# Seven block products for eight in the first output projection of a two-layer trunk kernel

## The reference

```python
# layer 0: y is the Fourier-mixed half of the input projection, z the other half
y = jnp.fft.fft2(ug, axes=(1, 3), norm='ortho').real.reshape(b, l, D_BRANCH)
o = (y * jax.nn.silu(z)) @ w_out            # (768 tokens x 2048) @ (2048 x 1024)
x = x + gt_l * o                            # ctx the same, with gt_c
# layer 1
h = rmsnorm(x, norm_g) * (1.0 + sc) + sh    # needs the sum over all 1024 features of x
q, k, v, z = split(h @ w_in)                # four heads; q and z of the latent tokens only
```

## Time and profile before

| | us |
|---|---|
| median of the runs | 947.4 |
| lowest of the runs | 945.88 |
| the profiled execution | 944.97 |
| its span, first to last instruction | 943.2 |
| PE busy in the span | 924.1 |
| granted PE clock, mean | 0.997 |

### The profile page before, as it was taken

One profiled execution on the slowest core, in us unless ns is written; L12 is line 12 of the kernel. 1 busy time (PEld: TensorE's weight loads), 2 busy tenths in 40 slices (PEclk: granted clock), 3 DMA queues, 4 the chain that ended last, 5 costly groups with the idle time before them and its releaser, 6 DMA issues.

```text
span 943.2 us, 13109 instructions
## 1 busy us (share of the span) xinstructions
PE 924.1 (98%) x4835; PEld 801.5 (85%) x4835; DVE 546.9 (58%) x813; ACT 351.0 (37%) x598; POOL 240.2 (25%) x243
## 2 busy tenths in 40 slices
PE   6999999999999999999999999999999999999996
PEld 6999998888888888888888888888888888888886
DVE  6897869999974422367444444435435445468333
ACT  8353343242232322354323334424323333354223
POOL 5259941746563000014100220012100221011001
PEclk9999999999999999999999999999999999999998
DMA  9762324555545212212211122202121121102222
GB/s 365 287 223 90 113 93 153 191 189 179 195 162 223 65 48 67 90 45 90 86 52 42 44 90 67 68 1 89 67 67 44 44 70 63 58 9 90 90 90 89
DMA packets 28747, 98.78 MB, mean 105 GB/s; under 512 B 3688, under 2 KB 5896, under 8 KB 28448
## 3 DMA queue, kind: packets, MB, share of 16 engines
q1 hardware_dynamic: 26688, 91.10, 28.2%
q0 software_dynamic: 1744, 6.84, 1.9%
q10 hardware_dynamic: 272, 0.26, 0.1%
HBM read 96.07 MB, written 2.10 MB: 104 GB/s over the span
## 4 chain that ended last, share of the span: by engine, by line
PE 89%; DVE 3%; DMA 2%; issue 2%; ACT 2%; POOL 1%; SPq 1%; POOLq 0%; DVEq 0%
PE banks L1725 29%; PE banks L1726 29%; PE banks L1727 29%; DMA raw<-stream 1%; DMA gate<-x_rows 1%; DVE hreg L1246 1%; ACT hreg L919 0%; POOL gate L661 0%; DVE wreg L1200 0%; DVE dist L1210 0%; PE banks L1852 0%; POOL gate L701 0%; DVE ring L1128 0%; PE banks L1870 0%; SPq L440 0%
## 5 line engine op out<-in xcount | busy, mean ns | idle before, releaser
L1725 PE MATMUL banks<-hreg,ring 128*128 128x512 f32 (+2 forms) x940 | 332.2, 353 | 1.9 <-DVE ring L1128 0.9
L1726 PE MATMUL banks<-hreg,ring 128*128 128x512 f32 (+2 forms) x940 | 331.3, 352 | 0.0
L1727 PE MATMUL banks<-hreg,ring 128*128 128x512 f32 (+2 forms) x940 | 329.5, 351 | 0.0
L1110 DVE TENSOR_TENSOR ring<-raw,ring 128x512 fp32r<-128x512 f32 x192 | 141.6, 751 | 244.3 <-ACT ring L713 243.0
L713 ACT ACTIVATE ring<-raw 128x512 fp32r<-128x512 f32 x192 | 118.7, 629 | 362.9 <-PE banks L1727 277.9
L1725 PEld LDWEIGHTS banks<-hreg,ring 128*128 128x128 f32 x940 | 177.3, 189 | 27.0 <-issue 3.6
L1727 PEld LDWEIGHTS banks<-hreg,ring 128*128 128x128 f32 x940 | 176.8, 188 | 22.4
L1726 PEld LDWEIGHTS banks<-hreg,ring 128*128 128x128 f32 x940 | 177.4, 189 | 21.1 <-issue 0.2
L628 POOL TENSOR_TENSOR gate<-xreg,gate 128x257 f32<-128x257 f32 (+1 forms) x64 | 69.2, 1111 | 78.4 <-ACT gate L862 62.2
L1142 DVE CUSTOM_DVE_ANT_0 dist<-raw,gate 128x1024 bf16<-128x1024 f32 x64 | 83.7, 1308 | 3.8
L661 POOL TENSOR_TENSOR gate<-gate 128x512 f32<-128x512 f32 x12 | 17.2, 1430 | 250.7 <-ACT gate L943 249.9
(11 more groups left out here) (230 smaller groups left out, 1095.0 us busy)
## 6 DMA issues: line engine op xcount, KB each, us to landing
raw<-stream SPq DMA_DIRECT2D x148, 512.0 KB, 3.3
gate<-stream SPq DMA_DIRECT2D x10, 512.0 KB, 11.2
gate<-x_rows SPq DMA_DIRECT2D x6, 512.0 KB, 6.8
gate<-x_lat POOLq DMA_DIRECT2D x1, 2048.0 KB, 8.8
xreg<-x_lat POOLq DMA_DIRECT2D x1, 2048.0 KB, 10.7
out<-xreg SPq DMA_DIRECT2D x3, 384.0 KB, 2.6
xreg<-stream SPq DMA_DIRECT2D x2, 512.0 KB, 11.1
gate<-cond_in SPq DMA_DIRECT2D x2, 512.0 KB, 10.8
```

Source lines behind the costliest of these rows:

```text
L1110: dve.tensor_tensor(ring[:, n % 2, 1, c], raw[:, buf, c], f32(ring[:, n % 2, 0, c]), ALU.subtract).then_inc(split_done, 1)
L1725: pe.matmul(out, left[0], right[0], start=start, stop=False)
L1726: pe.matmul(out, left[0], right[1], start=False, stop=False)
L1727: return pe.matmul(out, left[1], right[0], start=False, stop=stop)
```

## The change

Out0 becomes the seven products of Strassen's scheme. The weights are cut in 2 x 2 blocks by the parity of the output tile `m` and of the input tile `kk`. The gated values are cut by the parity of `kk` and by the halves of the 768 columns (384 each, so that the second half has 128 latent columns and all 256 of the context). A product q is the sum or difference of one or two weight blocks (first part of a row in `PRODUCTS`) times the sum or difference of one or two blocks of gated values (`RIGHT`; products 0 and 1 take a block as it is), and its result is added to or taken from one or two blocks of x (second part of the row). Each product has four output tile pairs i, so there are 28 units of one slot each. A unit is 8 `mm3` of 384 columns.

Three things feed a unit:

- **Weights.** Products 2 and 3 have one weight block. For 0, 1, 5 and 6 SP loads the first block and POOL issues a transfer that adds the second to it in the same buffer (`add_weights`). For product 4 the two blocks are loaded into two buffers and POOL subtracts the second from the first in two halves (`subtract_weights`). Then ACT and DVE split as before (`mix_hi`, `mix_lo`).
- **Gated values.** POOL makes 40 sums of 384 columns (`sum_right`) through two small buffers, ACT and DVE split each (`right_hi`, `right_lo`), at the units that `UNIT_STEPS` names: two at an odd one and three at an even one, from unit 3 to unit 18.
- **Results.** DVE adds each unit's result to x in two or more pieces (`evict`), two units later from unit 8 on.

The silu of the last two groups goes to a buffer of its own and group 7 is gated by DVE (`gate_last`). The context columns of x are complete before the latent ones, so their norm runs beside units 26 and 27, and head 0's context keys get two slots (`kc`) and matmuls of their own ahead of the head. Slots 4 and 5 of head 0 then have latent columns only.

```diff
+PRODUCTS = (
+    (((1, 0), (1, 1)), ((1, 0, 1), (1, 1, -1))),
+    (((0, 0), (0, 1)), ((0, 0, -1), (0, 1, 1))),
+    (((0, 0),), ((0, 1, 1), (1, 1, -1))),
+    (((1, 1),), ((0, 0, -1), (1, 0, 1))),
+    (((0, 0), (1, 1)), ((0, 0, 1), (1, 1, -1))),
+    (((0, 0), (1, 0)), ((1, 1, 1),)),
+    (((0, 1), (1, 1)), ((0, 0, 1),)),
+)
...
+RIGHT = {2: ((0, 1), (1, 1), ALU.subtract), 3: ((1, 0), (0, 0), ALU.subtract),
+         4: ((0, 0), (1, 1), ALU.add), 5: ((0, 0), (0, 1), ALU.add), 6: ((1, 0), (1, 1), ALU.add)}
+HOMES = (0, 1, 2, 3, 0, 2, 1)
+STEPS = [(q, i) for q in (2, 3, 4, 6, 5) for i in range(PAIRS)]
+UNIT_STEPS = [[] for _ in range(UNITS)]
+for _n in range(len(STEPS)):
+    UNIT_STEPS[3 + 2 * (_n // 5) + (_n % 5) // 2 - (_n % 5 == 4)].append(_n)
...
+FIRST_ORDER = [(i, k) for part in (range(6), range(6, PAIRS)) for i in range(4) for k in part]
+MIX_BANKS = (6, 7, 0, 1, 2, 3, 4, 5)
+EVICT_AT = {5: (0, 1), 6: (2, 3, 4), 7: (5,), **{_u: (_u - 2,) for _u in range(8, UNITS)}}
...
+            for n, (u, second) in enumerate(RAW_USES):
+                buf, _ = MIX_FIRST[u, second]
+                if n < RAW_BUFS:
+                    sp.wait_ge(split_done, 2 * (SLOT_OUT0 - RAW_BUFS + n) + 2 + SPLIT0)
+                else:
+                    v, was_second = RAW_USES[n - RAW_BUFS]
+                    if was_second:
+                        sp.wait_ge(mix_sum, 2 * (v - 4 * DIFFERENCE) + 2)
+                    else:
+                        sp.wait_ge(split_done, 2 * (SLOT_OUT0 + v) + 2 + SPLIT0)
...
+            def add_weights(u):
+                if u < UNITS and two_slots(u) and u // 4 != DIFFERENCE:
+                    buf, landed = MIX_FIRST[u, 0]
+                    pool.wait_ge(s_raw[buf], landed)
+                    pool.dma_start(raw[:, buf, :], mix_in[MIX_SLOTS.index((u, 1))],
+                                   accum_op=ALU.add).then_inc(s_added[buf], 16)
+            def subtract_weights(u):
+                if u // 4 == DIFFERENCE:
+                    (a, a_landed), (b, b_landed) = MIX_FIRST[u, 0], MIX_FIRST[u, 1]
+                    pool.wait_ge(s_raw[a], a_landed)
+                    pool.wait_ge(s_raw[b], b_landed)
+                    for c in (slice(0, SLOT // 2), slice(SLOT // 2, SLOT)):
+                        pool.tensor_tensor(raw[:, a, c], raw[:, a, c], raw[:, b, c],
+                                           ALU.subtract).then_inc(mix_sum, 1)
+            def sum_right(n):
+                q, i = STEPS[n]
+                (r0, h0), (r1, h1), op = RIGHT[q]
+                if n >= 2:
+                    pool.wait_ge(blo, n - 1)
+                pool.tensor_tensor(right_sum[n % 2], gate0[:, 2 * i + r0, MIX * h0:MIX * h0 + MIX],
+                                   gate0[:, 2 * i + r1, MIX * h1:MIX * h1 + MIX], op).then_inc(bsum, 1)
+            for p in range(GROUPS - 2):
...
-            pool.wait_ge(gated, 8 * GROUPS)
+            add_weights(0)
+            pool.wait_ge(dot_done, GROUPS)
+            gate_group(GROUPS - 2)
+            add_weights(1)
+            pool.wait_ge(gated_vec, 4)
+            for i in range(2):
+                pool.dma_start(y3[0:1, GROUPS - 1, NF * i:NF * i + NF],
+                               nyq_p[GROUPS - 1:GROUPS, :]).then_inc(s_row, 16)
+            pool.wait_ge(gated, 8 * (GROUPS - 1))
+            pool.wait_ge(gated_vec, 8)
             pool.dma_start(xl, x_lat).then_inc(s_xl2, 16)
             pool.dma_start(xc, x_ctx).then_inc(s_xc2, 16)
-            pool.wait_ge(dot_done, GROUPS)
+            pool.wait_ge(s_row, 32 * GROUPS)
+            for u in range(UNITS):
+                add_weights(u + 2)
+                subtract_weights(u + 1)
+                for n in UNIT_STEPS[u]:
+                    sum_right(n)
+                if u == 19:
+                    break
+            pool.wait_ge(blo, len(STEPS))
             pool.iota(dist[:, 0:896], pattern=[[1, 896]], base=-384, channel_multiplier=-1,
                       allow_small_or_imprecise_dtypes=True).then_inc(dist_set, 1)
+            pool.wait_ge(bsum, len(STEPS))
             pool.wait_ge(glo, FT)
             pool.dma_start(gate[:, TAIL + 1536:TAIL + 2560], rope_in).then_inc(s_rope, 16)
+            for u in range(20, UNITS):
+                add_weights(u + 2)
             pool.wait_ge(rstd_done, 1)
...
+            def mix_hi(u):
+                buf, landed = MIX_FIRST[u, 0]
+                act.wait_ge(s_raw[buf], landed)
+                if two_slots(u) and u // 4 != DIFFERENCE:
+                    act.wait_ge(s_added[buf], MIX_FULL[u][1])
+                for a in range(2):
+                    c = slice(a * SLOT // 2, (a + 1) * SLOT // 2)
+                    if u // 4 == DIFFERENCE:
+                        act.wait_ge(mix_sum, 2 * (u - 4 * DIFFERENCE) + a + 1)
+                    act.wait_ge(slot_done, 2 * (RING_OUT0 + u) + (a + 1 - 4 + DONE0))
+                    act.activation(ring[:, u % 2, 0, c], raw[:, buf, c], ACT.Copy).then_inc(hi_done, 1)
...
+            for u in range(1, UNITS):
+                mix_hi(u)
+                if u in (1, 2):
+                    group_hi(GROUPS - 3 + u)
+                for n in UNIT_STEPS[u]:
+                    right_hi(n)
...
+                src = mix_bank(u)
+                for r, half, sign in PRODUCTS[q][1]:
+                    m, factor = 2 * i + r, mod1 if sign > 0 else minus
+                    if half == 0:
+                        pieces = ((x3[:, m, 0:MIX], src, 0),)
+                    else:
+                        pieces = ((x3[:, m, MIX:LAT], src[:, 0:LAT - MIX], 0),
+                                  (xc3[:, m, :], src[:, LAT - MIX:], 1))
+                    for x, product, v in pieces:
+                        dve.scalar_tensor_tensor(out=x, in0=product, scalar=factor[:, m, v:v + 1], in1=x,
+                                                 op0=ALU.mult, op1=ALU.add).then_inc(mixed, 1)
...
+            gate_last(0)
+            for u in range(1, UNITS):
+                if u == 27:
+                    add_square(10)
+                    add_square(11)
+                mix_lo(u)
+                if u == 1:
+                    gate_last(1)
+                    group_lo(GROUPS - 2)
+                if u == 2:
+                    group_lo(GROUPS - 1)
+                for n in UNIT_STEPS[u]:
+                    right_lo(n)
+                if u == 4:
+                    columns(mod1[:, :, :], 16, 4 * KT, ((0, KT, bias0[:, 16:24]), (KT, 4 * KT, bias1)))
+                    multiplier(1, mod1[:, 2 * KT:3 * KT, :])
+                    link(dve.tensor_scalar(minus[:, :, :], mod1[:, 0:KT, :], -1.0, None, ALU.mult))
+                    dve.wait_ge(s_xl2, 16)
+                    dve.wait_ge(s_xc2, 16)
+                for v in EVICT_AT.get(u, ()):
+                    evict(v)
+                if u == 20:
+                    dve.wait_ge(bsum, len(STEPS))
...
+            add_square(12)
+            dve.wait_ge(root_done, 1)
+            dve.reciprocal(rstd_t[:, LAT:TOK], rstd_t[:, LAT:TOK]).then_inc(rstd_done, 1)
+            add_square(13)
+            for k in range(3):
+                h1_low(k, 1, LAT, TOK)
+            lo("kc", 0, RING_KC)
+            evict(26)
+            for k in range(3, KT):
+                h1_low(k, 1, LAT, TOK)
+            add_square(14)
+            evict(27)
...
+            def unit(u):
+                q, i = divmod(u, 4)
+                if u >= 8:
+                    pe.wait_ge(mixed, mixed_by(u - 8))
+                elif u >= 5:
+                    pe.wait_ge(z_done, 4 * GROUPS + 8)
+                for k in range(PAIRS):
+                    if k % 4 == 0:
+                        split(SLOT_OUT0 + u, k // 4)
+                    if i == 0:
+                        if q == 1:
+                            pe.wait_ge(glo, 2 * k + 2)
+                        else:
+                            pe.wait_ge(blo, STEPS.index((q, k)) + 1)
+                    last = mm3(mix_bank(u), part_of(u % 2, P * k), (right(q, k, 0), right(q, k, 1)),
+                               k == 0, k == PAIRS - 1)
+                    if k % 4 == 3:
+                        last.then_inc(slot_done, 1)
+                    if u == 26 and k == 4:
...
+            for n, (i, k) in enumerate(FIRST_ORDER):
+                if n % 4 == 0:
+                    split(SLOT_OUT0 + n // 8, n // 4 % 2)
+                pe.wait_ge(glo, 2 * k + 1)
...
+            pe.wait_ge(root_done, 1)
+            for k in range(KT):
+                if k % 2 == 0:
+                    split(SLOT_KC + k // 4, k // 2 % 2)
+                pe.wait_ge(hlo_done, KT + k + 1)
+                for tile in range(2):
+                    last = mm3(bank(3 + 2 * tile, CTX), part_of(k // 4, 2 * P * (k % 4) + P * tile),
+                               h_part(k, LAT, TOK), k == 0, k == KT - 1)
+                if k % 2:
+                    last.then_inc(slot_done, 1)
+                if k == 2:
```

(10 more changed lines are left out.)

495 lines of the change are left out of this document (262 added, 233 removed).

## The result

The changed kernel takes **1014.8 us** (median of four runs, 1013.9 to 1015.7) against 946.8 for the kernel before on the same chip: 1.073 times as long, 95% interval 1.072 to 1.074. The forecast was 1010. The profiled execution has a span of 1012.6 us, 69.4 more than before. One run of the kernel before took 1551 us and is left out of the ratio.

A forecast was written before the change was run, and what follows sets the result against it. PE, busy 98% of the span, was taken as the bound. Savings of 16.8 us against start, stalls and end gave +64.4, with extra hand-overs 65, so 945.0 us became 1010 us; range 970 to 1040.

The forecast's parts named there:

- What the matmuls save: Out0's matmuls: 117.6 us for 134.4 with 384-column products, 16.8 us less.
- The start: Start of out0: PE begins at 276.6 where it was 275.4, 1.2 us more.
- Unit 1: Second slot of out0: its adding transfer is issued late, behind group 6's gates on POOL; stall 8.5 us.
- Unit 2: Third slot of out0: its adding transfer queues behind the loads of x, served in order; stall 16.6 us.
- Units 4 to 15: Middle of out0: DVE becomes the bound through splits, sums of gated values and evictions; stall 16 us.
- Units 16 to 19: Product 4: load, subtraction, sums and split close a ring through one buffer, 40.8 us where PE needs 12.6; stall 28 us.
- Units 20 to 27: Last units of out0: unit 21's load waits for unit 19's split, then all run at PE's pace; stall 3.3 us.
- The end: From the last units into the head: waits for context norms 3.3 and token sums 3.9, head start 0.4; together 7.6 us.
- half clock: Rival: after long gaps PE's clock drops to 1.2 GHz, exposed at units 2 and 19 or 20; +8, 1018 us, chance 0.17.
- Slow adding transfers: Rival: adding transfers take 8 us, costing +21 at units 1, 2, 21 and eight others; 1035 us and up, chance 0.12.
- The queue is shared: Rival: POOL's queue keeps no order and other engines are quicker, unit 2 costing 6 us; 980 us, chance 0.15.
- PE stays fed: Rival: POOL has subtractions and sums done ahead, so PE never starves in out0; 936 us, not slower, chance 0.06.

The follow-up runs named there:

- e3_early_adds: Against the changed kernel, POOL issues the adding transfers for units 1, 2 and 3 earlier, ahead of the loads of x; 1010.4 us.
- e4_no_sums: Against the changed kernel, the 40 sums of gated values with their rounding and splits are left out, plain blocks used instead; 981.3 us.
- e12_three_sums: A third buffer for the sums of gated values, against a kernel with all order changes and later adding transfer for unit 20 (988.0 us); 980.8 us.
- e1_product4_added: Against the changed kernel, product 4's second weight block is added by a POOL transfer instead of loaded separately and subtracted; 992.7 us.
- e2_sums_first: Against the changed kernel, POOL makes a unit's sums of gated values ahead of the subtraction for the next unit; 1004.4 us.
- e8_result_in_second: Against the changed kernel, product 4's difference is written into the second block's buffer, not the first's; 1001.2 us.
- e5_second_plain: Against the changed kernel, POOL's transfers for second weight blocks overwrite the first block instead of adding to it; 1004.5 us.
- the four edits: Against the changed kernel: sums before subtractions, earlier adding transfers, difference in the second buffer, end reordered; alone 1004.4, 1010.4, 1001.2, 1010.2 us, together 990.3 us.

## Why the prediction was right

The forecast of 1010 us was 4.8 us low, and its sum of +65 stands against 69.4 in the profile. By its own steps:

- **What the matmuls save**, -16.8: right. A fed unit takes 4.16 us (49.9 / 12), 28 of them 116.4 where the forecast had 117.6, for 134.4.
- **The start**, +1.2: 0.8.
- **Unit 1**, 8.5: 5.5. The dots ended at 270.3, 2 us earlier than taken, and group 6's gates took 8.4 us, not 10.5, so that the adding transfer was issued at 278.88, not 282.8.
- **Unit 2**, 16.6: 11.1. x was issued at 288.0 and landed by 299.4, 11.4 us later, not 14.2; the split was at 302.8. The queue did keep order: three adding transfers issued at 289.04 landed up to 16.8 us later. `e3_early_adds` shows that this is the cause, but also that the wait moves on to slot 4. Slots 1 and 2 take 4.9 us more at the lower clock, which the sum had at nothing, and slot 4 waits 0.5. So the first four slots are 21.7 over their need, for 25.1.
- **Units 4 to 15**, 16: 16.3, and `e4_no_sums` shows that the sums are all of it. Inside it the halves differ. Less the 0.17 us of a matmul each, the waits ahead of units 5 to 7 are 7.5 us for 8, but those of the six pairs 4.4 for 8; the other 4.4 are units 5 and 7 at the lower clock, which used up time in which PE would have waited for DVE. The pair took 9.65 us, inside "9.0 to 10". The step named the missing third buffer for 1.4 us of a pair; that idle time is there, 1.47, but `e12_three_sums` shows that taking it away returns about 0.4.
- **Units 16 to 19**, 28: 28.8. The splits were 13.3, 11.5 and 15.1 us apart, for 13.5, 12.3 and 15. `e1_product4_added`, `e2_sums_first` and `e8_result_in_second` each open the ring where the step says that it closes.
- **Units 20 to 27**, 3.3: 7.7. This is the mis-sized term. The adding transfer was taken as 5 us; here its median was 8.1. `e5_second_plain` removes the addition and the stage's last part is 5.1 us shorter, 2.6 over PE's need. Another 1.7 us are the context squares inside unit 26, which the sum counts nowhere in this part.
- **The end**, 7.6: 10.9. The wait for the context norms was 3.2 for 3.3, and that for the token sums 2.75 for 3.9, with PE getting there 1.3 us later because of the clock. Behind that wait some 3 us more are the clock's: the context keys' matmuls lay 0.21 us apart and not 0.12, which the sum had not priced. (The step's own 9.3 less 5.8 is 3.5, not 3.3.)

So about 7.7 us too little for the last units and the end, and about 3.4 too much for the first slots, made the sum near. The stages and what feeds them were foreseen; that the total came within 5 us is in part luck. In the first slots alone the stalls were 25.1 forecast and 16.6 measured, and the clock, which the sum left out, gave 4.9 of that back. And the prediction names an adding transfer of over 7 us as a sign that it would be wrong. It took 7.9, and the forecast held only because most units wait for something else.

Of the rivals, **half clock** was right on the fact (0.60 and 0.61 in the windows behind the long waits). Two of its three hidden units, 1 and 17, were kept at 1.00 with no gain, as it says. Its 8 us at units 2 and 19 are not to be seen, since PE waits again at slot 4 and at unit 21, but no run kept the clock there. At the end, which it did not name, some 3 us are exposed. **Slow adding transfers** was right on the price, 7.9 us, and wrong on what it does: without the addition the time falls by 10.3 us, where the rival adds 21 (which from 1010 gives 1031, not its 1035). **The queue is shared** was refused by the landings behind x. **PE stays fed** gave 936 us; with the feed left out 940.6 was measured. The end gives 2.3 us of that (9.9 for 7.6), the stage 2.5 (120.1 for 117.6), with one wait over 1 us, 2.7 ahead of slot 2.

## What to carry to other kernels

A product scheme that saves an eighth of the matmuls is worth an eighth of one stage, here 1.8% of the kernel, and only if PE stays fed; what has to be counted first is the work per slot of all that feed it, since each slot now lasts half as long and asks for more. When PE was the bound with no waits, price the new feed as a ring: from one weight split to the next, everything that stands between in program order on any engine. Undoing one wait in such a chain gives back less than its length, for the next wait stands right behind it; the four edits here gave 33 us alone and 24 together.

## What was not expected of the hardware

- A transfer of 512 KB that adds on the way took 7.9 us in the median where the same one, plain, from the same queue took 4.9. POOL was held 0.90 us in the median for issuing it and 0.53 us for the plain one (a plain load of the same size between two adding ones, `rope_in`, 0.85), and the DMA engines were busier (0.91 for 0.64) while they moved less.
- DVE's half splits took 1.77 us a pair beside POOL's sums and 1.27 with POOL waiting, so letting POOL run ahead slowed the engine that was the bound.
- Throw-away matmuls in the waits kept the granted clock at 1.00 in two of five places where it had been 0.6, and did not change the time.
